# Matmuls of 480 columns for the high and the low part of 240 tokens, with their sums added behind, in a decoder step on one core

## The reference

```
h = modulate(rms_norm(x));  x += 0.5 * gate * swiglu(h)         # first FFN, inner width 2816
h = modulate(rms_norm(x));  z = h @ w_in
ca, cb, q, k, v, r, a_lr, g_conv, g_gla = split(z)
u = ca * sigmoid(cb);  d = causal_depthwise_conv(u, 31 taps)
y_conv = silu(layer_norm(d)) @ w_conv_out
o = gla(q, k, v, log_sigmoid(a_lr @ w_alpha + b) / 16)          # recurrence S_t = diag(a_t) S_(t-1) + k_t v_t
y_gla = (rms_norm(o) * silu(r)) @ w_gla_out
x += gate * ((sigmoid(g_conv) * y_conv + sigmoid(g_gla) * y_gla) @ w_out)
h = modulate(rms_norm(x));  x += 0.5 * gate * swiglu(h)         # second FFN
y = modulate(rms_norm(x))                                       # also the new conv and gla states
```

## Time and profile before

| | |
|---|---|
| median of 3 runs | 1433.17 us (1431.86 to 1433.81) |
| span of the profiled execution | 1432.1 us |
| TensorE busy | 1389.1 us, 97% |
| VectorE busy | 977.2 us, 68% |
| ScalarE busy | 539.3 us, 38% |
| chain that ended last | PE 84%, DVE 10%, ACT 3% |

### The profile page before, as it was taken

One profiled execution on the slowest core, in us unless ns is written; L12 is line 12 of the kernel. 1 busy time (PEld: TensorE's weight loads), 2 busy tenths in 40 slices (PEclk: granted clock), 3 DMA queues, 4 the chain that ended last, 5 costly groups with the idle time before them and its releaser, 6 DMA issues.

```text
span 1432.1 us, 28796 instructions
## 1 busy us (share of the span) xinstructions
PE 1389.1 (97%) x11782; PEld 1344.0 (94%) x11782; DVE 977.2 (68%) x1731; ACT 539.3 (38%) x797; POOL 80.2 (6%) x120
## 2 busy tenths in 40 slices
PE   6999999999999999999999999999999999999996
PEld 5899999999998999999899897999899999999996
DVE  6446675357547588998998997854554776456745
ACT  5423343224336222524243237422352344224433
POOL 6100000010001000000000000100000000000000
PEclk9999999999999999999999999999999999999998
DMA  9754646454364223213334453626312332323321
GB/s 322 237 177 155 205 149 206 147 168 142 103 208 142 89 88 93 89 60 104 125 128 146 136 169 127 220 91 198 104 59 74 92 117 89 114 76 106 101 77 60
DMA packets 132701, 189.49 MB, mean 132 GB/s; under 512 B 4621, under 2 KB 112545, under 8 KB 132386
## 3 DMA queue, kind: packets, MB, share of 16 engines
q1 hardware_dynamic: 111388, 112.54, 25.0%
q0 software_dynamic: 17136, 66.87, 14.0%
q10 hardware_dynamic: 4070, 8.57, 1.6%
HBM read 173.73 MB, written 15.18 MB: 132 GB/s over the span
## 4 chain that ended last, share of the span: by engine, by line
PE 84%; DVE 10%; ACT 3%; issue 2%; DMA 1%; POOL 0%; DVEq 0%; ACTq 0%
PE pu L646 51%; PE pu L828 13%; PE pu L817 11%; PE pu L660 2%; PE pg L690 2%; DVE w_lo L1680 1%; DMA work<-in_w_ada 1%; PE pg L1064 1%; ACT w_hi L1227 1%; DVE d L2106 1%; DVE w_lo L1969 1%; DVE work L2216 1%; PE pg L726 0%; DVE work L2215 0%; DVE work L2227 0%
## 5 line engine op out<-in xcount | busy, mean ns | idle before, releaser
L1680 DVE TENSOR_TENSOR w_lo<-raw,w_hi 128x1024 fp32r<-128x1024 f32 x152 | 186.1, 1225 | 255.5 <-ACT w_hi L1227 255.4
L1227 ACT CAST w_hi<-raw 128x1024 fp32r<-128x1024 f32 x152 | 158.9, 1046 | 412.0 <-PE pu L646 373.0
L646 PE MATMUL pu<-h_hi,w_hi 128*128 128x260 f32 x1408 | 288.4, 286 | 4.6 <-DVE work L2381 2.8
L646 PE MATMUL pu<-h_hi,w_lo 128*128 128x260 f32 x1408 | 284.1, 283 | 0.0
L646 PE MATMUL pu<-h_lo,w_hi 128*128 128x260 f32 x1408 | 283.3, 283 | 0.0
L646 PEld LDWEIGHTS pu<-h_hi,w_hi 128*128 128x128 f32 x1408 | 217.7, 189 | 8.7 <-DVE w_lo L1680 4.8
L646 PEld LDWEIGHTS pu<-h_hi,w_lo 128*128 128x128 f32 x1408 | 217.4, 189 | 0.0
L646 PEld LDWEIGHTS pu<-h_lo,w_hi 128*128 128x128 f32 x1408 | 217.2, 189 | 0.0
L2106 DVE SCALAR_TENSOR_TENSOR d<-u,cw,d 128x512 f32<-128x512 f32 x240 | 163.2, 745 | 0.1
L646 PE MATMUL pu<-f_hi,w_hi 128*128 128x260 f32 x704 | 142.9, 284 | 0.0
L646 PE MATMUL pu<-f_hi,w_lo 128*128 128x260 f32 x704 | 141.8, 283 | 0.0
(11 more groups left out here) (352 smaller groups left out, 2369.7 us busy)
## 6 DMA issues: line engine op xcount, KB each, us to landing
raw_a<-in_w_ada POOLq DMA_DIRECT2D x30, 1024.0 KB, 7.9
raw<-in_w_in SPq DMA_DIRECT2D x28, 1024.0 KB, 5.2
raw<-in_ffn_up SPq DMA_DIRECT2D x22, 1024.0 KB, 5.3
raw<-in_ffn_gate SPq DMA_DIRECT2D x21, 1024.0 KB, 5.3
raw<-in_ffn_down SPq DMA_DIRECT2D x16, 1024.0 KB, 5.1
gates_d<-sg ACTq DMA_DIRECT2D x24, 260.0 KB, 2.4
raw<-in_ffn_down SPq DMA_DIRECT2D x8, 768.0 KB, 4.4
work<-gates_d POOLq DMA_DIRECT2D x2, 2080.0 KB, 8.8
```

The costliest lines, as they stand in the source:

```text
L646: last = mm(pu[p][:, e, 0:HALF], w[p][:, k, :], m[:, k, e * HALF:(e + 1) * HALF], start=(k == 0 and j == 0), stop=(k == k_tiles - 1 and j ...
L1227: nc.scalar.copy(w_hi[p][:], raw[:, slot, :, p * P:(p + 1) * P]).then_inc(s_hi, 1)
L1680: V.tensor_tensor(w_lo[p][:], raw[:, slot, :, p * P:(p + 1) * P], w_hi[p][:].bitcast(F32), ALU.subtract).then_inc(s_lo, 1)
```

## The change

Each unit's columns are cut at 240 instead of 260. For the first 240 tokens, the products high x high and high x low have the same weights, and the two moving operands now lie in one tensor (`h_hl`, `f_hl`, `o_lh`), so one matmul of 480 columns makes both, side by side in one bank. The other 280 tokens are done as before, in the second bank, by three matmuls, and low x high of the first 240 by one. The two sums of the first 240 tokens are then joined outside TensorE: ScalarE copies the left one into `nb` (`near_part`), VectorE adds it to the right one in PSUM (`add_near`), and whoever reads the unit waits for that (`near_added`). The last units of down1_2, gates, out and down2_2 are not joined (`apart` gives None); they have six matmuls a row.

```diff
+NEAR = 240
+LEFT = 512 - NEAR
-        h_hi = sb("h_hi", [P, KT, N], F32R)
-        h_lo = sb("h_lo", [P, KT, N], F32R)
+        h_hl = sb("h_hl", [P, 2, KT, N], F32R)
+        h_hi, h_lo = h_hl[:, 0], h_hl[:, 1]
...
+        nb = sb("nb", [P, 2, NEAR])
...
+        def unit_psum(p, a=0, b=N):
+            return pu[p][:].rearrange("p e n -> p (e n)")[:, LEFT + a:LEFT + b]
...
+            end = min([v for v in at.values() if v > a] + [UNITS])
+            last = end - (a in (at["down1_2"], at["gates"], at["out"], at["down2_2"]))
...
@@ SyncE, GpSimd
-            sp.wait_ge(s_wz, 1)
-            sp.dma_start(wa[:, :, 0:RANK], ...).then_inc(s_wa, 16)
...
             pool.wait_ge(s_wz, 2)
+            pool.dma_start(wa[:, :, 0:RANK], ...).then_inc(s_wa, 16)
@@ TensorE
-            def unit(n, p, hi, lo, k_tiles=KT, ready=None, done=1):
+            def k_rows(p, wh, wl, hl, k, split, first, final):
+                hi, lo = (hl[:, j, k, :] for j in ((1, 0) if hl is o_lh else (0, 1)))
+                far = unit_psum(p, NEAR, N)
+                near = unit_psum(p, 0, NEAR)
+                if split:
+                    both = unit_psum(p, -NEAR, NEAR).rearrange("p (j n) -> p j n", j=2)
+                    mm(both, wh, hl[:, :, k, 0:NEAR], start=first, stop=False)
+                else:
+                    mm(near, wh, hi[:, 0:NEAR], start=first, stop=False)
+                mm(far, wh, hi[:, NEAR:N], start=first, stop=False)
+                if not split:
+                    mm(near, wh, lo[:, 0:NEAR], start=False, stop=False)
+                mm(far, wh, lo[:, NEAR:N], start=False, stop=False)
+                mm(near, wl, hi[:, 0:NEAR], start=False, stop=final)
+                return mm(far, wl, hi[:, NEAR:N], start=False, stop=final)
+
+            def unit(n, p, hl, k_tiles=KT, ready=None, done=1):
...
-                    for j, (w, m) in enumerate(((w_hi, hi), (w_hi, lo), (w_lo, hi))):
-                        for e in range(2):
-                            last = mm(pu[p][:, e, 0:HALF], w[p][:, k, :], m[:, k, e * HALF:(e + 1) * HALF],
-                                      start=(k == 0 and j == 0), stop=(k == k_tiles - 1 and j == 2))
+                    last = k_rows(p, w_hi[p][:, k, :], w_lo[p][:, k, :], hl, k, apart(n) is not None,
+                                  k == 0, k == k_tiles - 1)
@@ ScalarE
+            def near_part(p):
+                return nc.scalar.copy(nb[:, p, :], unit_psum(p, -NEAR, 0))
+            def near_added(n):
+                if apart(n) is not None:
+                    act.wait_ge(s_near, apart(n).value(1, 1))
-            def step(n, more=True):
+            def step(n, more=True, near=True):
                 act.wait_ge(s_done, n.value(1, 1))
+                if near and apart(n) is not None:
+                    near_part(n.base % 2).then_inc(s_nb, 1)
                 if more:
                     c = n.base % 4
                     split_hi(n + 2, c % 2, ((c + 2) // 2) % 2)
...
@@ ScalarE, v
-                    act.wait_ge(s_done, n.value(1, 1))
                     if c < 3:
                         step(n)
+                    else:
+                        act.wait_ge(s_done, n.value(1, 1))
+                        near_part(1).then_inc(s_nb, 1)
+                    near_added(n)
                     nc.scalar.copy(halves(sg[:, c, :]), psum(c % 2)).then_inc(s_evac[c % 2], 1)
                     if c == 3:
-                        step(n)
+                        step(n, near=False)
@@ VectorE
+            def add_near(p):
+                near = unit_psum(p, 0, NEAR)
+                return V.tensor_tensor(near, near, nb[:, p, :], ALU.add)
+            def add_near_of(n):
+                if apart(n) is not None:
+                    dve.wait_ge(s_nb, apart(n).value(1, 1))
+                    add_near(n.base % 2).then_inc(s_near, 1)
...
                 dve.wait_ge(s_done, n.value(1, 1))
+                if near:
+                    add_near_of(n)
                 if more:
@@ VectorE, residual
-                V.scalar_tensor_tensor(tile(x, m, 0, HALF), ps[:, 0, 0:HALF], g(0, 1), tile(x, m, 0, HALF),
+                near_added(n)
+                V.scalar_tensor_tensor(tile(x, m, 0, NP), unit_psum(p, 0, NP), g(0, 1), tile(x, m, 0, NP),
                                        ALU.mult, ALU.add)
-                V.scalar_tensor_tensor(tile(x, m, HALF, NP), ps[:, 1, 0:NP - HALF], g(0, 1), tile(x, m, HALF, NP),
-                                       ALU.mult, ALU.add)
...
@@ VectorE, up blocks of a turn
                             s = sg[:, k, :]
+                            dve.wait_ge(s_nb, apart_up(t, k) + 1)
+                            add_near(k).then_inc(s_near, 1)
                             dve.wait_ge(s_sg, 2 * t + 2)
+                            dve.wait_ge(s_near, apart_up(t, k) + 1)
```

More of the change, by code:

```diff
@@ L296, in decoder_step, with apart, apart_up @@
         pg = ctx.enter_context(nc.psum_tensor("pg", [P, 4, 512], F32))
+        def unit_psum(p, a=0, b=N):
+            return pu[p][:].rearrange("p e n -> p (e n)")[:, LEFT + a:LEFT + b]
+        def apart(n):
+            return next((n + off for a, b, off in APART if a <= n.base < b), None)
+        APART, off = [], 0
+        for a, ups in ([(at[f"{kind}1_{g}"], 2 * TURNS * (kind == "down" and g > 0))
+                           for kind, g in (("up", 0), ("down", 0), ("down", 1), ("down", 2))]
+                          + [(at[name], 0) for name in ("conv", "qk", "v", "gates", "yconv", "ygla", "out")]
+                          + [(at[f"{kind}2_{g}"], 2 * TURNS * (kind == "down" and g > 0))
+                             for kind, g in (("up", 0), ("down", 0), ("down", 1), ("down", 2))]):
+            end = min([v for v in at.values() if v > a] + [UNITS])
+            last = end - (a in (at["down1_2"], at["gates"], at["out"], at["down2_2"]))
+            off += ups
+            APART.append((a, last, off - a))
+            off += last - a
+        def apart_up(t, k):
+            n0 = at[f"down{1 + t // (2 * TURNS)}_{1 + t // TURNS % 2}"]
+            return apart(Lin(n0)).value() + 2 * (t % TURNS - TURNS) + k
         gates_d = nc.dram_tensor("gates_d", [3, KT, P, N], F32, kind="Internal").ap()
@@ L657, in rows @@
                     pe.wait_ge(s, v + k + 1)
-                    for j, (w, m) in enumerate(((w_hi, hi), (w_hi, lo), (w_lo, hi))):
-                        for e in range(2):
-                            last = mm(pu[p][:, e, 0:HALF], w[p][:, k, :], m[:, k, e * HALF:(e + 1) * HALF],
-                                      start=(k == 0 and j == 0), stop=(k == KT - 1 and j == 2))
+                    last = k_rows(p, w_hi[p][:, k, :], w_lo[p][:, k, :], hl, k, True, k == 0, k == KT - 1)
                     if k == KT - 1:
@@ L825, in up_unit @@
                     for k in range(4):
-                        for n, (w, m) in enumerate(((w_hi, h_hi), (w_hi, h_lo), (w_lo, h_hi))):
-                            for e in range(2):
-                                last = mm(pu[p][:, e, 0:HALF], w_block(w, j + half)[:, k, :],
-                                          m[:, 4 * half + k, e * HALF:(e + 1) * HALF],
-                                          start=(half == 0 and k == 0 and n == 0), stop=(half == 1 and k == 3 and n == 2))
+                        last = k_rows(p, w_block(w_hi, j + half)[:, k, :], w_block(w_lo, j + half)[:, k, :], h_hl,
+                                      4 * half + k, True, half == 0 and k == 0, half == 1 and k == 3)
                     last.then_inc(s_bd, 1)
@@ L918, in ffn @@
                                 late_transposes(4, 5)
-                            unit_pair(Lin(n0), h_hi, h_lo, s_h, (which - 1) * 3 * KT, rest if which == 1 else None,
+                            unit_pair(Lin(n0), h_hl, s_h, (which - 1) * 3 * KT, rest if which == 1 else None,
                                       KT if which == 1 else 5)
@@ L931, in ffn @@
                         last.then_inc(s_lt, 1)
-                    if which == 2 and g == 2:
+                    if g == 2:
                         for c in range(KT):
@@ L935, in ffn @@
                                 pe.wait_ge(s_um, 2 * TURNS * (2 * (which - 1) + g) - 1 + c)
-                            unit(Lin(at["down2_2"] + c), c % 2, f_hi, f_lo, GROUPS[g],
+                            unit(Lin(at[f"down{which}_2"] + c), c % 2, f_hl, GROUPS[g],
                                  ready=(s_a, a0, GROUPS[g] - 1) if c == 0 else None)
-                            if c:
+                            if c and which == 2:
                                 y_transposes(c - 1)
@@ L1135, in _ @@
                 for s in range(6):
-                    unit(Lin(at["gates"] + 6 * hh + s), s % 2, h_hi, h_lo)
+                    unit(Lin(at["gates"] + 6 * hh + s), s % 2, h_hl)
                     if s == 1:
@@ L1195, in _ @@
             for c in range(2, 4):
-                unit(Lin(at["yconv"] + c), c % 2, h_hi, h_lo)
```

(10 more changed lines are left out.)

81 lines of the change are left out of this document (47 added, 34 removed).

## The result

The changed kernel takes 1449.34 us (1448.70 to 1449.67, 4 runs) against 1433.49 of the kernel before beside it: ratio 1.0114, 95% interval 1.0102 to 1.0126. The profiled execution spans 1448.0 us. The prediction was 1434, its range 1420 to 1446, so the time lies outside. The first question is where 16 us went; the second why TensorE, with 1408 matmuls fewer, gave so little back.

The account below looks back on a forecast made before the run. TensorE, busy 97% of the span at 120.1 ns per 260-column unit matmul, was taken to bound the kernel. 1432.1 - 13.5 saved + 14.2 of delays = 1432.8 us span, so 1434 measured; range 1420 to 1446.

Parts of the forecast that it names:

- The failed step: Unit matmuls: 11.8 ns fixed in each, one matmul fewer a row, 11 ns a row saved, -13.5 us in sum.
- The cut: 240-column unit matmul: 111.8 ns stands at its 111 ns weight load, so another 0.5 ns lost.
- R1: Rival, unit matmuls: the extra time goes by columns, only 3 ns a row saved, 1444 us; chance 0.20.
- R4: Rival, unit matmuls: load-bound pace makes the 480 free, 38 ns a row saved, 1401 us; chance 0.04.
- v: v units: transposes wait for additions behind VectorE's taps, 4.4 us late in one half, 2.5 in the second; +7.0 us.
- Heads: Heads: later VectorE merges, 1.2 us each in first and third, 0.8 in the two with some slack; +4.0 us.
- yconv: yconv units: VectorE is packed and TensorE waits for it, three or four additions; +1.4 us.
- ygla to out: Last ygla unit is split and out starts on its tile: copy and addition, +0.8 us.
- Seams: Four seams from down to the half-size turns: later copy, shorter residual, late end of up units; +1.0 us.
- Load of w_a, straight code: w_a's load moved to POOL's queue: nothing; two-turn loops made straight code: nothing, or a few tenths.
- VectorE over 98% in 590 to 660: Sign in the end of q/k and the v units: VectorE busy over 98% of that window.
- The rule given for what would show it: Sign in the unit rows: 480-column matmuls start 212 ns before the next if fixed part, 222 if by columns.

Follow-up runs that it names:

- probe: Changed kernel plus a tail of TensorE alone, blocks of 16 matmuls of one size each: 129.6 ns at 280 columns, 216.5 at 480; whole time some 60 us longer.
- whole_all: Changed kernel with no unit split: six matmuls a row of 240 and 280 columns, no copy and no addition; 1439.07 us.
- no_join: Changed kernel with all units split but without ScalarE's copies, VectorE's additions and the waits for them; outputs lack one product; 1428.89 us.
- whole_260: Changed kernel with no unit split, no copy, no addition, and the cut at 260 columns again instead of 240; 1432.24 us.

## Why the prediction was wrong, step by step

The medians add up to a ledger, each step one kernel against the next (the kernel before, run beside each, had medians of 1433.5 to 1433.8; the first step is not clear of noise):

```
before                                  1433.5
cut at 260, everything else changed     1432.2    -1.2
cut at 240, six matmuls a row           1439.1    +6.8
five matmuls a row, no join             1428.9   -10.2
ScalarE's copies                        1434.4    +5.5
VectorE's additions                     1449.3   +15.0
```

**The failed step** is the term "If the 11.8 ns are a fixed part of each, a row falls from 720.6 to 650 + 5 x 11.8 = 709 ns". It was to give 13.5 us; TensorE gave 4.8. The 8.7 us between are over half of the error. The steps behind it were observations of other forms and of the lower clock, and neither could tell a part by columns from a fixed one at full rate. No second size in this form stood in the trace of before, as the prediction said; it then took all of the 11.8 ns as fixed. By the probe's 280 and 480 columns some 8 are. Dropping a matmul at the same cut gave 7.2 ns a row (whole_all against no_join, 10.2 us over 1408 rows), where the term had 11.8 less 0.5.

**The cut** took most of that back. The prediction gave the 240-column matmul 0.5 ns for its load, and nothing for the uneven cut itself. It costs 3 to 4 ns in the middle of a stretch and 4.7 a row on average (6.8 us over all 1440 rows). What is left, 4.8 us over 1408 rows, is 3.4 ns a row. R1, cost by columns, had 3, but that is partly luck: it had no fixed part and no price for the cut, and the two nearly cancel. R4's 38 ns a row stand without a working; a 480-column matmul that takes 216 ns rules it out in any case.

**v**, +7.0. The waits were foreseen well: 4.97 where 0.73 stood, so 4.2 against 4.4, and 2.0 against 2.5; one for w_lo (1.06) came on top. The 4.3 us of lower clock behind them were not in the sum. The kernel before could have shown that a wait of this kind can cost the clock: behind its wait of 2.0 us in yconv the clock stands at 0.72, just behind the end of the window that the prediction read the earlier trace rows. Window of the kernel before:

```profile
924.00:930.00 6.00, 5.84 (x36) 5.88 (x37) 5.71 (x9) 0.63 (x1) 0.00 (x0) 0.72 0.39 117
```

**Heads**, +4.0: 4.8, of which two waits of 0.8 in the heads that were to have slack. L1064's wait (now L1100's) grew to 6.5 us, within the 6 to 7 named. **yconv**, +1.4: 1.4, by luck, since it is the clock and not the additions. **ygla to out**, +0.8: 0.3. **Seams**, +1.0: about 2, since the half-size turns wait a little at each. **Load of w_a, straight code**, nothing: confirmed by whole_260.

**VectorE over 98% in 590 to 660**: a miss, 62.95 of 70 us, less than the 66.00 before, with ten additions there and not twelve. Where TensorE stands, VectorE soon stands too: here for the cast, which is behind the delayed copy (1.60 us at 633.00). A packed engine doesn't show as more packed when the loop it sits in gets longer.

The rule given for what would show it (480 columns at 212 or 222 ns) read 216, about half way, and half way is what it is: a fixed part of some 8 ns and the rest by columns. It took the 130 at 280 columns beside it to tell.

Left open: why 240 and 280 in turn cost 3 ns a row more than 260 and 260, why 512 columns lie 3 ns above the other sizes, and when a wait of about 2 us or a cluster of shorter ones costs the clock. Of VectorE adding straight from both halves of PSUM nothing can be said; it wasn't tried.

## What to carry to other kernels

A time by matmul is split into a part by columns and a fixed part only by rows at two sizes in the same form. If the trace has one size, both ends stay in the sum with equal weight, and the gain of "fewer, longer matmuls" is taken from the smaller end. Here the truth lay between them, and the uneven cut, which neither end had, took most of the gain. An operation that is added to a queue engine costs its place, not its length: 0.41 us behind the taps became 4.2 us of waiting. And a long wait of TensorE is priced with what follows at half clock: here 1.4 to 2.9 us behind each wait of 2.5 us and more, while those of about 2 us cost it only in some kernels.
